# Fewer tokens through the dense experts: 342 dense columns for 352, three chunks between heads for four, one transfer for preactivations and gates

## The chip, the cores and the metric

The kernel runs on one core of a Trainium2 chip. The metric is the device time of one execution in microseconds (us); the number given for a kernel is the median of its runs. PE is TensorE, DVE VectorE, ACT ScalarE, POOL GpSimd and SP SyncE.

## What is computed

One layer of a decoder over 512 tokens of width 2048, in float32. A combined projection feeds latent attention and a spatial gating unit; their output is added to the residual stream h. Then come 16,384 single-neuron experts chosen by product keys, a gated projection of layer inputs, and a last norm. The experts take two thirds of the time:

```python
def peer(a, w_q, k1, k2, u_exp, v_exp):           # a = rmsnorm(h), 512 tokens
    q = (a @ w_q)                                  # 8 heads, two halves of 128
    t1, i1 = top_k(q[first half] @ k1.T, 16);  t2, i2 = top_k(q[second half] @ k2.T, 16)
    top, sel = top_k(t1[:, None] + t2[None, :], 16)
    experts, gates = index(i1 * 128 + i2, sel), softmax(top)   # 8 heads x 16 picks a token
    return sum_k(gates * gelu(u_exp[experts] . a) * v_exp[experts])
h = h + sigmoid(rmsnorm(h) @ W_gate) * (p @ W_ple)
```

## The kernel before, in words

Activations lie transposed, tokens along the free dimension. Each float32 operand is split into a high and a low part (aH and aL, wH and wL), and each product is three matmuls (lines 1745 to 1747). Weights come in pieces of 1 MB: SP loads them into raw, ACT makes wH (line 626), DVE makes wL = raw - wH (line 1048), both in two buffers. A 128 x 2048 piece is a slot of 48 matmuls.

The tokens are handled in three ways. The first TD = 352 go through all experts densely: 128 u chunks of 128 experts each (one slot each, matmuls of 352 columns), then the values in NGROUPS = 16 groups of GROUP = 8 chunks, one group being eight slots. For these tokens a table gates in HBM holds one gate for each expert and token; POOL fills it with zeros early (line 507, 22 transfers) and adds the gates of each head by indirect transfers of one column (line 540, 48 for a head, 384 in all). DVE scales a finished u chunk into ut (line 1472), ACT applies gelu and stores it to pre in HBM. For the values SP loads the chunk and its gates (two transfers, pre_in and gate_in), POOL multiplies (line 585), ACT and DVE split it into actH (line 882) and actL (line 1580).

The last 128 tokens (A) and the 32 before them (B) go by rows instead: for each pick the rows of u and v of one expert a token are gathered, 128 rows at once. The 32 tokens of B are laid out in four sets on the 128 partitions, so that their 128 picks make 32 (B_PICKS), 160 with the 128 of A. Picks below U_PICKS = 64 fall in the u stage, where one gather brings u and v (line 557, 2 MB); the others in the value stage (lines 569 and 577, 1 MB each). For each pick DVE forms the dot product with the token's activations (line 1552; those of A lie in PSUM, those of B in SBUF as b_tok), ACT applies gelu and the gate (lines 899 and 903), and DVE adds the weighted row of v to hT (line 1563) or to b_acc (line 1568). u_step and v_step give each chunk or slot its share of these operations, two to a pick. In the u stage POOL issues four adds of gates after each gather; ADDS_FIRST = 164 adds precede the first one.

The order of each engine's work is written out by hand and engines wait on semaphores. In the head stage a head has two slots of query projection (512 columns), key scores, and HEAD_U = 4 u chunks; DVE's retrieve interleaves the top-16 searches with wL and the scaling. After the heads come 96 more u chunks; picks begin at chunk FIRST_PICK = ROUTE_U + 4 and, but for the last four, end before chunk LAST_PICK = 118. In the value groups ACT seeds PSUM with h (seed) and brings it back (unload); in the first and last group DVE adds PSUM to h (accumulate, line 1585). In the last group PE waits for all picks behind its first slot, transposes the rows of A back, sums the four sets of B by a product with sel behind the second, and squares for the ple norm follow on ACT and DVE. The projection of p (16 tiles) and the gate tiles end the kernel.

Of the kernel before, what the change touches and what calls it, by code (L numbers as in the profile page):

```python
# [22 lines left out]
P = 128  # L23
# [12 lines left out]
BT = 32  # L36
TA = T - P
TD = TA - BT
# [3 lines left out]
B_PICKS = A_PICKS // SETS  # L42
# [10 lines left out]
FIRST_SLOT = 2  # L53

# [8 lines left out]
def v_step(g, q):  # L63

    slots = GROUP * (NGROUPS - 1) - FIRST_SLOT
    return 2 * U_PICKS + max(0, GROUP * g + q - FIRST_SLOT) * 2 * (PICKS - U_PICKS) // slots
# [37 lines left out]
NSLOTS = _n  # L104

# [47 lines left out]
def trunk_layer(nc, a, stream, out, gates_dram, pre_dram):  # L153
# [59 lines left out]
    projT = at("projT", [KD, T], F, W0 + 16 * KB)
# [29 lines left out]
    gates_r = at("gates_r", [NT, P], F, C0)  # L243
    idx_d = at("idx_d", [NTD, P], U32, C0 + 2 * KB)
    idx_s = at("idx_s", [P], U32, C0 + 2 * KB + 1536)
    pre_in = [at(f"pre_in{i}", [TD], F, C0 + 2 * KB * i) for i in range(2)]
    gate_in = [at(f"gate_in{i}", [TD], F, C0 + 4 * KB + 1536 * i) for i in range(2)]
# [6 lines left out]
    gates_b = at("gates_b", [B_PICKS], F, C0 + 14 * KB + 1472)  # L254
    dots_b = at("dots_b", [B_PICKS], F, C0 + 12 * KB + 704)
    pick_wb = at("pick_wb", [B_PICKS], F, C0 + 14 * KB + 1600)
    sel = at("sel", [BT], F, C0 + 14 * KB + 1728)
# [17 lines left out]
    with ctx:  # L275
# [34 lines left out]
        pre_loaded = [sem(f"pre_loaded{i}") for i in range(2)]  # L310
# [7 lines left out]
        gates_loaded = [sem(f"gates_loaded{i}") for i in range(2)]  # L318
# [4 lines left out]
        row_landed = [sem(f"row_landed{i}") for i in range(5)]  # L323
        v_row_landed = [sem(f"v_row_landed{i}") for i in range(2)]
        dot_done, dot_gelu, pick_weighed, pick_done = sem("dot_done"), sem("dot_gelu"), sem("pick_weighed"), sem("pick_done")
        b_loaded, rep_ready, b_tok_done, b_tok_early, b_tok_ready = (
# [1892 lines left out]
```

## Time and profile before

| | us |
|---|---|
| Median of 3 runs (lowest, highest) | 3009.12 (2995.46, 3012.29) |
| The profiled execution, its own time | 2995.07 |
| Its span, first to last instruction | 2992.9 |
| PE busy | 2950.2 (99%) |
| PE loading weights | 2771.6 (93%) |
| DVE busy | 2220.2 (74%) |
| POOL busy | 1435.3 (48%) |
| ACT busy | 1255.1 (42%) |

The core moved 798.01 MB, 267 GB/s over the span. The granted clock of TensorE was 0.998 of its full 2.4 GHz. Busy time of PE counts any moment with a matmul under way; matmuls overlap, so the sum of their durations is larger than it. A row's number with "<-" behind "idle before" names what ended the idle time.

### The profile page before, as it was taken

The page shows a single profiled execution, that of the slowest core. Times are in us where ns is not written, and L with a number is a line of the kernel's source. Part 1 is how long each engine was busy: PE and PEld are TensorE (multiplying, and loading weights), DVE is VectorE, ACT ScalarE, POOL GpSimd, SP SyncE. Part 2 cuts the span into 40 slices and gives each one's busy share as a digit, 9 for nine tenths or more (in the row PEclk, how much of TensorE's full clock was granted, in tenths as well). Part 3 has the DMA queues.
Part 4 walks back from the last instruction along what each step waited for, and adds up shares of the span by engine and source line. Part 5 has one row for each costly group of instructions (what it writes and reads, how often), then busy time and mean ns, then how long its engine had stood idle before and what let it go on. Part 6 is the DMA issues. An engine that isn't in the chain of part 4 may idle for free. (4 is left out here: it accounts for less than half of the span.)

```text
span 2992.9 us, 43288 instructions
## 1 busy us (share of the span) xinstructions
PE 2950.2 (99%) x16888; PEld 2771.6 (93%) x16888; DVE 2220.2 (74%) x2801; ACT 1255.1 (42%) x1818; POOL 1435.3 (48%) x813
## 2 busy tenths in 40 slices
PE   9999999999999999999999999999999999999998
PEld 7888668889999999999999999999999999999787
DVE  5465664578878777777777669888888888986445
ACT  5224542333333333333333334555555555554422
POOL 1010000008888888888888125665555667660000
PEclk9999999999999999999999999999999999999999
DMA  8462222235445599999999889999999999994222
GB/s 297 169 241 86 71 85 98 99 123 125 128 125 137 132 338 339 361 354 364 358 349 362 329 306 412 406 410 403 407 410 408 402 407 401 400 381 152 97 96 99
DMA packets 205172, 798.01 MB, mean 267 GB/s; under 512 B 68208, under 2 KB 121472, under 8 KB 128736
## 3 DMA queue, kind: packets, MB, share of 16 engines
q1 hardware_dynamic: 90768, 405.36, 36.2%
q0 software_dynamic: 95440, 367.63, 34.0%
q10 hardware_dynamic: 18816, 23.11, 2.2%
q8 instruction: 85, 1.39, 0.2%
q14 instruction: 63, 0.52, 0.0%
HBM read 745.46 MB, written 50.51 MB: 266 GB/s over the span
## 5 line engine op out<-in xcount | busy, mean ns | idle before, releaser
L1745 PE MATMUL ps<-aH,wH 128*128 128x352 f32 (+2 forms) x3088 | 1062.0, 344 | 6.9 <-DVE wL L1048 6.9
L1747 PE MATMUL ps<-aH,wL 128*128 128x352 f32 (+2 forms) x3088 | 1059.1, 343 | 0.0
L1746 PE MATMUL ps<-aL,wH 128*128 128x352 f32 (+2 forms) x3088 | 1059.0, 343 | 0.0
L1048 DVE TENSOR_TENSOR wL<-raw,wH 128x2048 fp32r<-128x2048 f32 x333 | 787.5, 2365 | 224.6 <-ACT wH L626 221.9
L540 POOL DMA_INDIRECT gates<-gates_r,idx_d x384 | 753.9, 1963 | 377.9 <-DVE gates_r L1463 243.0
L626 ACT ACTIVATE wH<-raw 128x2048 fp32r<-128x2048 f32 x333 | 636.8, 1912 | 677.2 <-PE ps L1747 581.2
L1745 PE MATMUL ps<-actH,wH 128*128 128x352 f32 x2048 | 662.2, 323 | 3.2 <-DVE wL L1048 3.2
L1747 PE MATMUL ps<-actH,wL 128*128 128x352 f32 x2048 | 661.9, 323 | 0.0
L1746 PE MATMUL ps<-actL,wH 128*128 128x352 f32 x2048 | 661.4, 323 | 0.0
L1745 PEld LDWEIGHTS ps<-aH,wH 128*128 128x128 f32 x3088 | 581.2, 188 | 47.8 <-DVE wL L1048 6.6
L1747 PEld LDWEIGHTS ps<-aH,wL 128*128 128x128 f32 x3088 | 580.9, 188 | 38.1
L1746 PEld LDWEIGHTS ps<-aL,wH 128*128 128x128 f32 x3088 | 580.3, 188 | 38.4 <-issue 0.7
L1745 PEld LDWEIGHTS ps<-actH,wH 128*128 128x128 f32 x2048 | 385.9, 188 | 4.9 <-DVE wL L1048 4.8
L1746 PEld LDWEIGHTS ps<-actL,wH 128*128 128x128 f32 x2048 | 385.4, 188 | 0.0
L1747 PEld LDWEIGHTS ps<-actH,wL 128*128 128x128 f32 x2048 | 385.4, 188 | 0.0
L585 POOL TENSOR_TENSOR pre_in<-pre_in,gate_in 128x352 f32<-128x352 f32 x128 | 221.9, 1735 | 279.3 <-DMA gate_in<-gates 278.2
L1552 DVE SCALAR_TENSOR_TENSOR rows<-rows,ps 128x2048 f32<-128x2048 f32 x128 | 291.8, 2280 | 26.7 <-DMA rows<-uv_rows,idx_s 20.2
L1563 DVE SCALAR_TENSOR_TENSOR hT<-rows,pick_w,hT 128x2048 f32<-128x2048 f32 x128 | 308.5, 2410 | 0.7 <-ACT pick_w L903 0.7
L1472 DVE TENSOR_TENSOR ut<-ps,rstd 128x352 f32<-128x352 f32 x128 | 67.0, 524 | 152.0 <-PE ps L1747 117.1
L569 POOL DMA_INDIRECT rows<-u_rows,idx_s x64 | 121.1, 1892 | 41.9 <-DVE rows L1552 19.0
L1580 DVE TENSOR_TENSOR actL<-pre_in,actH 128x352 fp32r<-128x352 f32 x128 | 68.0, 531 | 89.4 <-ACT actH L882 67.6
L557 POOL DMA_INDIRECT rows<-uv_rows,idx_s x64 | 82.4, 1288 | 105.2 <-DVE hT L1563 87.9
(273 smaller groups left out, 2433.2 us busy)
## 6 DMA issues: line engine op xcount, KB each, us to landing
raw<-s_pu SPq DMA_DIRECT2D x128, 1024.0 KB
raw<-s_pv SPq DMA_DIRECT2D x128, 1024.0 KB
gates<-zeros POOLq DMA_DIRECT2D x22, 1024.0 KB, 8.6
pre<-ut ACTq DMA_DIRECT2D x128, 176.0 KB
pre_in<-pre SPq DMA_DIRECT2D x128, 176.0 KB
gate_in<-gates SPq DMA_DIRECT2D x128, 176.0 KB
raw<-s_out SPq DMA_DIRECT2D x16, 1024.0 KB
raw<-s_pq SPq DMA_DIRECT2D x16, 1024.0 KB
```

The lines of the kernel that those rows point to most:

```text
L540: pool.indirect_dma_start(out=gates_flat, out_offset=bass.IndirectOffsetOnAxis(ap=idx_d[0:m, t, c:c + 1], axis=0), in_=gates_r[0:m, t, c:c ...
L557: pool.indirect_dma_start(out=rows[ROW_AT[j]][:, :, :].rearrange("p a d -> p (a d)"), out_offset=None, in_=a["uv_rows"], in_offset=bass.In ...
L569: pool.indirect_dma_start(out=rows[ROW_AT[j]][:, 0, :], out_offset=None, in_=a["u_rows"], in_offset=bass.IndirectOffsetOnAxis(ap=ids_of(j) ...
L585: nc.gpsimd.tensor_tensor(pre_in[b][:, :], pre_in[b][:, :], gate_in[b][:, :], ALU.mult).then_inc(act_gated, 1)
L626: A(wH[parity][:, :], raw[at_n][:, :], ACT.Copy).then_inc(hi_ready, 1)
L1048: V.tensor_tensor(wL[parity][:, :], src[:, :], wH[parity][:, :].bitcast(F), ALU.subtract).then_inc(lo_ready, 1)
L1552: V.scalar_tensor_tensor(r3, r3, 1.0, act_of, ALU.mult, ALU.mult, accum_out=d).then_inc(dot_done, 1)
L1563: V.scalar_tensor_tensor(hT[:, :, TA:T], v3, pick_w[:, j:j + 1], hT[:, :, TA:T], ALU.mult, ALU.add).then_inc(pick_done, 1)
L1580: V.tensor_tensor(actL[b][:, j, 0:TD], src[:, :], actH[b][:, j, 0:TD].bitcast(F), ALU.subtract).then_inc(act_wlo, 1)
L1745: mm(out, wh, xh, start=start, stop=False, skip_group_check=skip_group_check)
L1746: mm(out, wh, xl, start=False, stop=False, skip_group_check=skip_group_check)
L1747: return mm(out, wl, xh, start=False, stop=stop, skip_group_check=skip_group_check)
```

## The change

- BT goes from 32 to 42: the B tokens become 42, TD = 342, and 170 tokens go by rows. Three sets of 42 fill 126 partitions, the 128 picks of B make 43 (the last set has 42; idx_b and gates_b are cleared for the missing one). PICKS is 171.
- HEAD_U goes from 4 to 3: 24 chunks lie between the heads, 104 behind them. The weight buffers then alternate by head (slot_at, chunk_at).
- 70 picks in the u stage, ADDS_FIRST = 126. Six picks, the last of A, move behind B's: they lie in the last value group and the first projection tiles (tail_steps, TAIL = 6), the last five in a row buffer of their own.
- gates and pre become one tensor pair in HBM with a pitch of 352 for each; SP brings a chunk's gates and preactivations by one transfer. The zeros cover the whole tensor, 44 transfers.
- The last group is seeded and unloaded by ACT like the others. The sum over B's sets is formed in four of its tiles, in PSUM columns behind the 342. The transposes back move into the second half of the projection, and the ple squares and splits of the last 128 tokens come after them, apart from the rest.
- b_tok is taken out of early columns in two steps behind a wait for the last u chunk; sel is built later; buffers in SBUF are laid out anew.

```diff
-BT = 32
+BT = 42
 TA = T - P
+PW = 352
...
-B_PICKS = A_PICKS // SETS
+B_PICKS = -(-A_PICKS // SETS)
+SPAN = SETS * BT
...
-HEAD_U = 4
+HEAD_U = 3
 ROUTE_U = HEAD_U * HEADS
-ADDS_FIRST = 164
+ADDS_FIRST = 126
 FIRST_PICK, LAST_PICK = ROUTE_U + 4, KEYS - GROUP - 2
-U_PICKS, LATE = 64, 4
+U_PICKS, LATE = 70, 4
+TAIL = 6
 FIRST_SLOT = 2
+MAIN = PICKS - TAIL
+FIRST_B = A_PICKS - TAIL
...
+def tail_steps(h):
+
+    if h < 2:
+        return [2 * MAIN + h]
+    return [2 * (MAIN + h // 3) + h % 3] if h >= 3 and h % 3 < 2 and h // 3 < TAIL else []
...
-    _at = _j % 3 if _j < U_PICKS - LATE else 2 if _j < U_PICKS else 3 + _j % 2
+    if _j < U_PICKS:
+        _at = _j % 3 if _j < U_PICKS - LATE else 2
+    else:
+        _at = 4 - (MAIN - _j) % 2 if _j <= MAIN else 5
...
-                sp.dma_start(pre_in[b][:, :], pre_dram[c, :, :]).then_inc(pre_loaded[b], 16)
-                sp.dma_start(gate_in[b][:, :], gates_rows[:, c, :]).then_inc(gates_loaded[b], 16)
+                sp.dma_start(pair_in[b][:, :], pair_rows[:, c, 0:PW + TD]).then_inc(pair_loaded[b], 16)
...
-            fills = -(-KEYS * TD // 2048)
...
+            fills = KEYS * 2 * PW // 2048
...
-                m = min(P, TD - t * P)
+                m = min(P, PW - t * P)
...
-                    pool.wait_ge(b_tok_ready, 1)
-                if j == A_PICKS:
+                    pool.wait_ge(tile_done, CUM[S0["pv"] - 1])
+                if j == FIRST_B:
                     pool.wait_ge(b_loaded, 32 * SETS)
+                if j == MAIN + 1:
+                    pool.wait_ge(tile_done, CUM[S0["pv"] + GROUP * (NGROUPS - 1) - 1])
...
-                pool.wait_ge(pre_loaded[b], (c - b) * 8 + 16)
-                pool.wait_ge(gates_loaded[b], (c - b) * 8 + 16)
-                nc.gpsimd.tensor_tensor(pre_in[b][:, :], pre_in[b][:, :], gate_in[b][:, :], ALU.mult).then_inc(act_gated, 1)
+                pool.wait_ge(pair_loaded[b], (c - b) * 8 + 16)
+                nc.gpsimd.tensor_tensor(pre_in[b], pre_in[b], gate_in[b], ALU.mult).then_inc(act_gated, 1)
...
+            for j in range(MAIN + 1, PICKS):
+                gather_u(j)
+                gather_v(j)
...
+                if KD * (NGROUPS - 1) + 1 <= v <= KD * (NGROUPS - 1) + 4:
+                    A(ps[:, 4 + k % 4, TD:TD + 4 * BT].rearrange("p (c t) -> p c t", c=4), hT[:, 4 * k - 4:4 * k, TD:TA],
+                      ACT.Copy, scale=0.0)
...
                 act.wait_ge(h_acc, v)
+                if g == NGROUPS - 1 and 1 <= k <= 4:
+                    A(b_sum[:, 4 * k - 4:4 * k, :], ps[:, 4 + k % 4, TD:TD + 4 * BT].rearrange("p (c t) -> p c t", c=4),
+                      ACT.Copy).then_inc(b_copied, 1)
...
-                if KD <= v < KD * (NGROUPS - 1):
+                if KD <= v:
                     unload(v)
-                if KD <= v + 4 < KD * (NGROUPS - 1):
+                if KD <= v + 4 < KD * NGROUPS:
                     seed(v + 4)
...
-                if q == 1:
-                    for r in range(4):
-                        act.wait_ge(back_done, r + 1)
-                        A(hT[:, 4 * r:4 * r + 4, TA:T], ps[:, BACK[r], :].rearrange("p (a b) -> p a b", a=4),
-                          ACT.Copy).then_inc(back_copied, 1)
-                    act.wait_ge(back_copied, 4)
+                for o in tail_steps(2 * q) + tail_steps(2 * q + 1):
+                    if o % 2 == 0:
+                        weigh_pick(o // 2)
...
+                    if (s, m) == (1, 3):
+                        for r in range(4):
+                            act.wait_ge(back_done, r + 1)
+                            A(hT[:, 4 * r:4 * r + 4, TA:T], ps[:, BACK[r], :].rearrange("p (a b) -> p a b", a=4),
+                              ACT.Copy).then_inc(back_copied, 1)
+                    if s == 1 and m >= 4:
+                        for k in range(4 * m - 16, 4 * m - 12):
+                            late_hi(k)
+            A(late_sq[:, :, :], hT[:, :, TA:T], ACT.Square).then_inc(sq_ready, 1)
...
-                scale_chunk(uc + 1, 1, at_n(3))
+                if HEAD_U > 2:
+                    scale_chunk(uc + 1, chunk_at(b, 1), at_n(3))
                 key_indices(h, 1)
                 pair_sums(h)
-                lo(n + 5, 1)
+                if HEAD_U > 2:
+                    lo(n + 5, slot_at(b, 5))
                 pair_maxima(h)
-                scale_chunk(uc + 2, 0, at_n(4))
+                if HEAD_U > 3:
+                    scale_chunk(uc + 2, chunk_at(b, 2), at_n(4))
                 pair_more(h)
-                lo(n + 6, 0)
+                if HEAD_U > 3:
+                    lo(n + 6, slot_at(b, 6))
...
+                for o in tail_steps(2 * q):
+                    pick_step(o)
                 lo(m + 1, (q + 1) % 2)
+                for o in tail_steps(2 * q + 1):
+                    pick_step(o)
...
+                if q == 2:
+                    dve.wait_ge(b_copied, 4)
+                    dve.wait_ge(h_acc, KD * (NGROUPS - 1))
+                    V.tensor_tensor(hT[:, :, TD:TA], hT[:, :, TD:TA], b_sum[:, :, :], ALU.add).then_inc(b_added, 1)
+                    dve.wait_ge(b_added, 1)
...
+            for h in range(16, 3 * TAIL):
+                for o in tail_steps(h):
+                    pick_step(o)
+            lo(S0["gate"], 0)
+            for k in range(KD):
+                late_lo(k)
+            n = N_SQ["ple"] + KD
+            dve.wait_ge(sq_ready, n + 1)
+            dve.wait_ge(sq_added, n)
+            V.tensor_reduce(ssum[:, TA:T], late_sq[:, :, :].rearrange("p k t -> p t k"), AX, ALU.add).then_inc(sq_added, 1)
+            lo(S0["gate"] + 1, 1)
...
-                seeded = 0 < g < NGROUPS - 1
+                seeded = g > 0
...
+                    if g == NGROUPS - 1 and 1 <= k <= 4:
+                        if k == 1:
+                            pe.wait_ge(pick_done, MAIN)
+                            pe.wait_ge(sel_ready, 1)
+                        for c in range(4):
+                            t = TD + c * BT
+                            ins = mm(ps[:, 4 + k % 4, t:t + BT], b_acc[:, 4 * k - 4 + c, :], sel[:, :], start=False, stop=True,
+                                     skip_group_check=True)
...
-                if q == 0:
-                    pe.wait_ge(pick_done, PICKS)
-                    for k in range(KD):
-                        ins = nc.tensor.transpose(ps[:, BACK[k // 4], (k % 4) * P:(k % 4 + 1) * P], hT[:, k, TA:T], ident[:, :])
-                        if k % 4 == 3:
-                            ins.then_inc(back_done, 1)
-                if q == 1:
-                    pe.wait_ge(back_copied, 1)
-                    pe.wait_ge(sel_ready, 1)
-                    for k in range(KD):
-                        ins = mm(ps[:, BACK[0], k * BT:(k + 1) * BT], b_acc[:, k, :], sel[:, :], start=True, stop=True)
-                    ins.then_inc(b_sum_done, 1)
-
...
+                    if (s, m) == (1, 3):
+                        pe.wait_ge(pick_done, PICKS)
+                        for k in range(KD):
+                            ins = nc.tensor.transpose(ps[:, BACK[k // 4], (k % 4) * P:(k % 4 + 1) * P], hT[:, k, TA:T], ident[:, :])
+                            if k % 4 == 3:
+                                ins.then_inc(back_done, 1)
+            pe.wait_ge(back_copied, 4)
+            tile(S0["gate"], 0, 0, waits=N_SC["ple"] + KD)
+            norm_sum("ple", 2)
             tile(S0["gate"] + 1, 1, 1)
```

## Rows read from the trace of the kernel before

**Rows 1.** Windows: us; PE, PEld, DVE, ACT, POOL busy; clock; DMA share, GB/s
```profile
620.00:1040.00 420.00, 420.00 (x2392) 393.61 (x2393) 346.56 (x1111) 140.44 (x145) 310.19 (x156) 1.00 0.49 130
1040.00:1400.00 360.00, 358.95 (x2243) 358.66 (x2242) 275.44 (x200) 125.36 (x162) 301.32 (x167) 1.00 0.98 345
1780.00:2200.00 420.00, 417.78 (x2607) 417.05 (x2606) 361.47 (x254) 226.61 (x382) 235.57 (x142) 1.00 1.01 405
2715.00:2775.00 60.00, 59.01 (x383) 58.60 (x381) 38.20 (x46) 32.22 (x40) 0.00 (x0) 1.00 0.34 118
2775.00:2800.00 25.00, 22.73 (x96) 17.89 (x97) 15.16 (x15) 16.08 (x23) 0.00 (x0) 1.00 0.29 101
```

**Rows 2.** Timeline of PE (start, us): first and last of 57, 27, 27 matmuls
```profile
2929.78 0.39 PE L1745 MATMUL ps<-aH,wH 128*128 128x512 f32 x1
...
2942.47 0.39 PE L1747 MATMUL ps<-aH,wL 128*128 128x512 f32 x1
...
2199.70 0.32 PE L1746 MATMUL ps<-actL,wH 128*128 128x352 f32 x1
...
2203.86 0.32 PE L1745 MATMUL ps<-actH,wH 128*128 128x352 f32 x1
...
2964.77 0.28 PE L1745 MATMUL ps<-aH,wH 128*128 128x256 f32 x1
...
2967.89 0.28 PE L1747 MATMUL ps<-aH,wL 128*128 128x256 f32 x1
```

**Rows 3.** Groups of instructions by line and shape, whole span
```profile
L1745 PE MATMUL ps<-actH,wH 128*128 128x352 f32 x2048 | 662.2, 323 | 3.2 <-DVE wL L1048 3.2
L1745 PE MATMUL ps<-aH,wH 128*128 128x352 f32 x2048 | 662.1, 323 | 2.9 <-DVE wL L1048 2.9
...
L507 POOL DMA_DIRECT2D gates<-zeros x22 | 19.6, 890 | 69.0 <-DMA gates<-zeros 68.7 <-POOL zeros L499 0.3
...
L1585 DVE TENSOR_TENSOR hT<-hT,ps 128x352 f32<-128x352 f32 x32 | 16.0, 514 | 7.9 <-PE ps L1747 7.8
```

**Rows 4.** Timeline of DVE where the head loop turns
```profile
817.17 0.23 DVE L1432 CAST best_kf<-best_k 128x128 f32<-128x128 uint32 x1
820.58 0.52 DVE L1472 TENSOR_TENSOR ut<-ps,rstd 128x352 f32<-128x352 f32 x1 [3.18 <-issue]
```

**Rows 5.** Timeline of ACT (ScalarE) there
```profile
827.17 0.60 ACT L850 ACTIVATE pqT<-ps 128x512 f32<-128x512 f32 x1 [5.53 <-PE ps L1747]
```

**Rows 6.** Groups of POOL's instructions from 1200 to 1640 us
```profile
L540 POOL DMA_INDIRECT gates<-gates_r,idx_d x168 | 321.6, 1914 | 57.1 <-issue 50.8 <-DMA gates<-gates_r,idx_d 6.3
L557 POOL DMA_INDIRECT rows<-uv_rows,idx_s x42 | 50.5, 1204 | 12.8 <-issue 12.8
```

**Rows 7.** Waits of DVE from 1060 to 1705 us: us in total, times, longest
```profile
DVE rows L1552 <- DMA rows<-uv_rows,idx_s: 19.3, 16, 3.7
```

**Rows 8.** Timeline of POOL, three adds of gates
```profile
1165.60 2.46 POOL L540 DMA_INDIRECT gates<-gates_r,idx_d  x1 [0.30 <-issue]
1168.36 1.55 POOL L540 DMA_INDIRECT gates<-gates_r,idx_d  x1 [0.30 <-issue]
1170.21 3.30 POOL L540 DMA_INDIRECT gates<-gates_r,idx_d  x1 [0.30 <-issue]
```

**Rows 9.** Timeline of DVE over the same stretch
```profile
1164.33 2.28 DVE L1048 TENSOR_TENSOR wL<-raw,wH 128x2048 fp32r<-128x2048 f32 x1
1166.54 2.28 DVE L1552 SCALAR_TENSOR_TENSOR rows<-rows,ps 128x2048 f32<-128x2048 f32 x1
...
1169.76 2.35 DVE L1563 SCALAR_TENSOR_TENSOR hT<-rows,pick_w,hT 128x2048 f32<-128x2048 f32 x1
```

**Rows 10.** Timeline of POOL: transfer after the zeros, first add, first gather
```profile
327.79 0.57 POOL L521 DMA_DIRECT2D hT<-x  x1 [108.81 <-DVE qT L1247]
...
674.14 1.67 POOL L540 DMA_INDIRECT gates<-gates_r,idx_d  x1 [242.95 <-DVE gates_r L1463]
...
1060.98 1.01 POOL L557 DMA_INDIRECT rows<-uv_rows,idx_s  x1 [0.30 <-issue]
```

More of the change, by code:

```diff
@@ L104, with slot_at, chunk_at @@
 NSLOTS = _n
+def slot_at(b, j):
+    return ((2 + HEAD_U) * b + j) % 2
+def chunk_at(b, j):
+    return (HEAD_U * b + j) % 2
 def raw_at(n):
@@ L309, in trunk_layer @@
         pre_stored = [sem(f"pre_stored{i}") for i in range(2)]
-        pre_loaded = [sem(f"pre_loaded{i}") for i in range(2)]
+        pair_loaded = [sem(f"pair_loaded{i}") for i in range(2)]
         g_scaled = sem("g_scaled")
@@ L392, in _, with load_head @@
                     load(S0["out"] + 2 * i + j, stream["out"][2 * i + j, :, :], j)
-            def load_head(h):
+            def load_head(h, b):
                 n = S0["head"] + (2 + HEAD_U) * h
                 for s in range(2):
-                    load(n + s, stream["pq"][2 * h + s, :, :], s)
+                    load(n + s, stream["pq"][2 * h + s, :, :], slot_at(b, s))
                 for s in range(HEAD_U):
-                    load(n + 2 + s, stream["pu"][HEAD_U * h + s, :, :], s % 2)
-            with sp.Fori(0, HEADS) as h:
-                load_head(h)
+                    load(n + 2 + s, stream["pu"][HEAD_U * h + s, :, :], slot_at(b, 2 + s))
+            with sp.Fori(0, HEADS // 2) as i:
+                for b in range(2):
+                    load_head(2 * i + b, b)
             nu = S0["pu"] - ROUTE_U
@@ L881, in weight_hi @@
                 act.wait_ge(act_gated, c + 1)
-                A(actH[b][:, j, 0:TD], src[:, :], ACT.Copy).then_inc(act_whi, 1)
+                A(actH[b][:, j, 0:TD], src, ACT.Copy).then_inc(act_whi, 1)
             u_beat(ROUTE_U, 0, nu + ROUTE_U, 0)
@@ L965, in v_beat, with dense_square @@
                 turn(KD * g + 2 * q)
+            def dense_square(k):
+                act.wait_ge(h_acc, KD * (NGROUPS - 1) + k + 1)
+                act.wait_ge(sq_added, N_SQ["ple"] + k - 1)
+                A(sq[k % 2][:, 0:TA], hT[:, k, 0:TA], ACT.Square).then_inc(sq_ready, 1)
+                A(aH[:, k, 0:TA], hT[:, k, 0:TA], ACT.Copy, scale=gain("ple", k)).then_inc(act_hi, 1)
             for q in range(GROUP):
@@ L2016, in head_slots @@
                         pe.wait_ge(pq_copied, 2 * h + s - 1)
-                    tile(n + s, s, s, waits=N_SC["ffn"] if first and s == 0 else None)
+                    tile(n + s, slot_at(b, s), s, waits=N_SC["ffn"] if first and s == 0 else None)
                     if first:
@@ L2031, in head_slots @@
                                 ins.then_inc(b_tok_done, 1)
-                    u_slot(n + 2 + s, s % 2, HEAD_U * h + s, s, first=first and s == 1)
+                    u_slot(n + 2 + s, slot_at(b, 2 + s), HEAD_U * h + s, chunk_at(b, s), first=first and s == 1)
             head_slots(0, 0, first=True)
```

231 lines of the change are left out of this document (125 added, 106 removed).

## The prediction

> **What bounds the kernel now.** I read the page first, then the windows by stage. [rows 1] put the stages side by side: the eight heads with four chunks each (620 to 1040 us), the 96 other u chunks (to 1780), the value groups, of which the last ends at 2775, and the projection. The reader is to see that PE is busy for all of 420 us in the heads, for 358.95 of 360 in the u chunks and 417.78 of 420 in the value groups: PE bounds them all. But three others stand close behind. DVE is at 83% in the heads and at 86% in the value groups, POOL at 84% in the u chunks, and the DMA share is 0.98 there and 1.01 in the value groups. So the question is less what PE saves than who can follow it.
>
> **What PE saves.** The timeline of PE gives a matmul's price by the distance of starts, not by its duration, since neighbours overlap [rows 2]. 512 columns: 2929.78 to 2942.47 over 56 distances, 226.6 ns. 352 columns: 4.16 us over 26, 160.0 ns. 256 columns: 3.12 us over 26, 120.0 ns. A column costs (226.6 - 120.0)/256 = 0.416 ns; 256 plus 96 columns gives 160.0, which is the middle row, so the line is straight. 342 columns make 155.8 ns. [rows 3] count 2048 matmuls with aH and 2048 with actH at 352 columns, and each stands for three: 12,288. Times 4.17 ns that is **-51.2 us**. A slot of 48 goes from 7.68 to 7.48 us. Below nothing this can't go; it is nothing if columns cost in blocks of 32, which the three shapes (all multiples of 32) don't exclude.
>
> PE's work for the 42 split tokens stays: 16 products with sel and 16 transposes before and after, in other places.
>
> **Heads (three chunks between two).** No chunk is dropped, only moved behind the heads, so PE pays the same. A head gets shorter by one slot and three times 0.2, 8.3 us; DVE sheds one wL (2.28) and one scaling (about 0.5). At the end of a head it is then 5.5 us further behind PE. Now it ends a head at 817.40, waits 3.18 us for issue where its loop turns, scales a chunk from 820.58 [rows 4] and then has wL (2.28) written at 823.3; PE needs that at 827.17, where ScalarE sees the first query tile end [rows 5]: 3.9 us to spare. So it comes 1.6 us late in the three turns of the loop, and elsewhere, without the 3.18, in time: **+4 us** (0 to 10; DVE has 73 us idle in 420 now [rows 1], half of it left).
>
> **POOL between 1040 and 1780.** This is the term that decides. It issues one gather (2 MB) for each pick and four adds of gates. In 440 us of steady work [rows 6] it did 168 adds of 1.914 us and 42 gathers of 1.204 with 70 us between them, nearly all "issue": 442 us, it never rests. That is 440/42 = 10.5 us for a pick. Today's plan spreads 60 picks over 82 slots of 7.68, one in 10.5 us: a tie, and [rows 7] show it as a tie, DVE waiting 16 times for rows in the whole stage (19.3 us, none longer than 3.7, hidden in its own idle time). The new plan spreads 66 picks over 90 slots of 7.48, one in 10.2 us, still with four adds each (258 adds are left after the first 126, so they last for 64.5 picks, the whole stage). POOL is short of 0.3 us in each pick.
>
> Why POOL is so slow is in the two timelines [rows 8, 9]. An add takes 1.55 us under the dot product of 1166.54, which reads one input from PSUM. The one of 1165.60 takes 2.46: wL runs until 1166.61, which leaves 1.45. The one of 1170.21 takes 3.30: the row addition runs until 1172.11, which leaves 1.40. So an instruction of POOL that starts under a DVE operation with two SBUF inputs waits for its end. The Trainium skill, "GPSIMD Engine Reference", section Specifications, says that its SBUF interfaces contend with DVE instructions that have two SBUF inputs; the trace agrees, with the 2.46 and 3.30 against 1.55.
>
> The price: the lead that POOL has at the start is about one pick (two gathers go before the first adds) and DVE may be some 3 us late before PE feels it, together 13 us. Loss = 64 x (p - 10.2) - 13 for a pace of p. At today's p = 10.53 (4 x 1.914 + 1.204 + 5 x 0.305 + a rare wait for the adds of a head) 8 us. With the adds at the 2.36 us that they take apart in the heads (674.14 to 1060.98 for 164 [rows 10]) p = 10.95, 35 us. I take p = 10.65, **+16 us**, nearer to the stage's own rows but above them, as the DVE operations with two SBUF inputs take the same 4.0 us out of a shorter slot. It ends with the adds, at about the 116th of 128 chunks.
>
> **The zeros.** 44 fills instead of 22, the 22 new ones behind the others. A fill costs POOL 0.9 us and 3.1 of waiting (19.6 + 69.0 over 22 [rows 3]), so they take 89 us, and POOL idles there for 108.81 us before its next transfer [rows 10]. That idle time is the cover. **0 us**, to 3 without cover.
>
> **The value groups.** One transfer for two leaves 128 packets of 2776 B for 256 of 1408 B. POOL, ACT and DVE do as much as before with 3% fewer columns. Bytes for a slot: 405 GB/s x 7.68 us = 3.11 MB now [rows 1]; some 0.02 MB less after, for 165 picks of which 95 lie in 118 slots. 3.09 MB in 7.48 us are 413 GB/s. What the queues can carry beyond 405 no row shows; cost from 0 to, if 405 is the most, 118 x (7.63 - 7.48) = 18 us. I take **+2**, since PE lost only 2.2 us in 420 at 405 GB/s and a share of 1.01. The Trainium skill, "DMA: Bandwidth & Descriptors", puts the ceiling of the SBUF fabric at 435 GB/s, and a core's share of HBM at about 358. The first would leave the stage free, the second would forbid even now's 405; the trace decides against the second.
>
> **The end.** Six picks (12 operations of 2.28 or 2.35) move into the last group; ACT takes over 16 additions of 0.51 [rows 3]; squares and low parts shrink by a quarter of some 12 us. DVE had 38.20 of 60 us [rows 1]: 38.2 + 28 - 8.2 - 3 = 55, of 59.8, with more than a slot's 7.48 bunched in slots 2, 3 and 6. A late wL there costs 2 to 3 us. Behind, the transposes move from slot 1 of the group to the middle of the projection, where they wait for the last pick; by the plan it comes after eight slots, two squares, a wL and itself, at 70 us of the group, and is wanted after eight slots and twelve tiles of six matmuls, at 76. Queued behind that wait on PE are four projection tiles and the gate. PE now loses 1.0 + 2.3 us there and this partly stays. **+3 us** (-2 to 12).
>
> **Sum.** The profiled execution took 2995.07 us (span 2992.9, 2.2 around it): 2995.1 - 51.2 + 4 + 16 + 0 + 2 + 3 = 2969.9. The median of the runs is 14 us above that execution. A part of this may be the very race of POOL and DVE, already counted; I carry 6 over: **2976 us**.
>
> **Rivals.**
> - *All of the saving arrives.* POOL's stalls fall so that it follows at 10.2. For it: an unhindered add takes 1.55 and a gather 1.0, 8.7 us in all. Against it: [rows 6], where it had every reason to be faster and wasn't. 2995 - 51 + 9 = 2953, to 2962 with the shift of the median. Chance 0.2.
> - *DMA is the bound in the value groups* on top of my case: +16 more, 2992. For it a share of 1.01; against it PE's 417.78 of 420 at that share. 0.1.
> - *Slower: POOL falls out of step.* A start at random finds DVE in such an operation for 54% of a slot, with half of 2.3 us to wait: 0.6 us for each of five instructions, p = 8.7 + 3.0 = 11.7, a loss of 83 us in place of 16: 3043. It decides (over 3024) from p = 11.4. For it: the alignment that gives 10.5 belongs to slots of 7.68. Against it: waiting behind an operation is itself what aligns. 0.1. A pace between 10.9 and 11.3 leaves 2990 to 3020, no change: 0.05.
> - *The columns don't count singly* (blocks of 32): no gain, and no loss on POOL either as the slots stay: 2995 + 5 + 6 = 3006. 0.05.
>
> **How the numbers follow.** My case has 0.5, from 2955 to 2992. A measurement of this kernel can tell about 0.5%, 15 us around 3009: faster is below 2994. Faster: 0.47 of mine, 0.2 and 0.03 of the DMA case, 0.70. Slower: 0.10. No change: 0.20. The range that leaves 2 in 10 outside is 2950 to 3010; it takes in the free case below and most of the no-change cases above.
>
> **What the profile after would show.** Distances of 155.8 ns at 342 columns. Between the last head and the last eight u chunks, PE losing 10 to 20 us where it now loses 3, behind wL, with DVE waiting for rows far more than 19.3 us and POOL still without rest at 10.5 to 10.8 us for a pick. In the value groups a GB/s of about 410 and slots of 7.5. A loss of 1 to 2 us in each turn of the head loop. Wrong would be: no wait of PE in the u stage at all (free case), slots of 7.6 in the value groups (DMA), over 11.3 us for a pick (slower), or distances of 160.

## The result, and the profile after

The changed kernel took 3010.98 us (median of 20 runs, 3003.15 to 3023.38), the one before, measured side by side with it, 3001.12 (20 runs, 2995.25 to 3012.29): ratio 1.0032, 95% interval 1.0022 to 1.0042. That is 10 us slower: a small loss, but the interval leaves 1 out. It lies above my 2976 and above the upper end of my range, 3010. The profiled execution of after took 3012.23 us (span 3010.5) against 2995.07 (span 2992.9): 17 us more.

Busy time of the engines in the changed kernel (from here on: after), and then its windows in the order of [rows 1]:
```profile
PE 2935.2 (98%) x16888; PEld 2752.4 (91%) x16888; DVE 2270.8 (75%) x2836; ACT 1270.5 (42%) x1898; POOL 1481.4 (49%) x853
```
```profile
620.00:1040.00 420.00, 412.00 (x2358) 383.90 (x2357) 364.56 (x1130) 143.02 (x153) 278.69 (x145) 1.00 0.52 148
1040.00:1400.00 360.00, 350.44 (x2196) 349.77 (x2195) 273.66 (x192) 121.08 (x159) 289.33 (x164) 0.99 0.98 346
1780.00:2200.00 420.00, 418.19 (x2648) 417.41 (x2647) 361.56 (x256) 222.37 (x376) 240.53 (x138) 1.00 0.99 403
2715.00:2775.00 60.00, 59.35 (x386) 59.06 (x385) 52.05 (x45) 41.48 (x79) 14.40 (x10) 1.00 0.79 298
2775.00:2800.00 25.00, 21.53 (x109) 19.04 (x108) 19.87 (x22) 14.01 (x27) 4.43 (x2) 0.93 0.58 211
```
PE was busy all of the heads and 358.95 of 360 us in the u chunks; now it is idle for 8 of 420 and 9.56 of 360. The value groups are as full as before. So the loss lies ahead of 1780 us. Who is late there, from the waits of 1060 to 1705 us (total, times, longest), which answer to [rows 7]:
```profile
DVE rows L1632 <- DMA rows<-uv_rows,idx_s: 65.6, 26, 10.0
...
POOL pair L576 <- DMA pair<-gates_r,idx_d: 31.7, 4, 9.8
...
PE ps L1851 <- DVE wL L1121: 25.6, 6, 7.4
```
PE waits for wL, DVE before it for gathered rows, and POOL, which issues the gathers, for adds of gates: four times here and a fifth time before 1591.39, 10.85 us that the view puts under "issue" though they stand at the same place of the program:
```profile
1591.39 2.82 POOL L576 DMA_INDIRECT pair<-gates_r,idx_d  x1 [10.85 <-issue]
```
That makes five waits of 6.5 to 10.8 us, 42.5 in all. POOL's groups from 1200 to 1640 us, beside [rows 6]:
```profile
L576 POOL DMA_INDIRECT pair<-gates_r,idx_d x161 | 303.9, 1888 | 76.6 <-issue 59.0 <-DMA pair<-gates_r,idx_d 17.6
L594 POOL DMA_INDIRECT rows<-uv_rows,idx_s x41 | 50.5, 1232 | 12.5 <-issue 12.5
```
An add takes 1.888 us, 1.914 before; what has grown is the wait for adds, from 6.3 to 28.4 (17.6 and the 10.8 that stand under "issue"). For a gather with its adds POOL takes (303.9 + 76.6 + 50.5 + 12.5)/41 = 443.5/41 = 10.8 us.

Where the 17.6 us of span went, from the starts of PE's matmuls. I call a distance of starts above 0.6 us, less the 0.16 of a matmul, a hole, and the excess over 0.16 of those from 0.27 to 0.6 slow. Stages in us; holes and slow in brackets:
```
           heads, from     u chunks, to     value groups   last group,
           606 us on       the first value  0 to 14        projection, gate
before     429.2 (2, 0)    744.5 (3, 0)     927.2 (4, 0)   275.6
after      372.7 (9, 1)    829.6 (30, 9)    912.8 (3, 1)   279.0
```
The chunk that left each head's gap reappears in the u stage, so the first two stages go together: 1173.7 before, 1202.3 after, **+28.6**. Value groups **-14.4**, the rest **+3.4**; sum 17.6.

One of the four long holes (of 4.9, 5.0, 7.6 and 5.0 us; each follows one of the last four waits), at the start of the seventh head's adds. Timeline of POOL (start, us, engine, operation, in brackets the idle time before it and who ended it), then DVE, then PE:
```profile
1442.73 0.99 POOL L594 DMA_INDIRECT rows<-uv_rows,idx_s  x1 [0.31 <-issue]
1444.02 1.45 POOL L576 DMA_INDIRECT pair<-gates_r,idx_d  x1 [0.30 <-issue]
1445.78 1.42 POOL L576 DMA_INDIRECT pair<-gates_r,idx_d  x1 [0.30 <-issue]
1456.99 2.40 POOL L576 DMA_INDIRECT pair<-gates_r,idx_d  x1 [9.78 <-DMA pair<-gates_r,idx_d]
1459.69 3.38 POOL L576 DMA_INDIRECT pair<-gates_r,idx_d  x1 [0.30 <-issue]
1463.37 1.34 POOL L594 DMA_INDIRECT rows<-uv_rows,idx_s  x1 [0.30 <-issue]
```
```profile
1461.57 2.29 DVE L1121 TENSOR_TENSOR wL<-raw,wH 128x2048 fp32r<-128x2048 f32 x1
1473.89 2.29 DVE L1632 SCALAR_TENSOR_TENSOR rows<-rows,ps 128x2048 f32<-128x2048 f32 x1 [10.04 <-DMA rows<-uv_rows,idx_s]
```
```profile
1473.67 0.32 PE L1853 MATMUL ps<-aH,wL 128*128 128x342 f32 x1
1481.39 0.65 PE L1851 MATMUL ps<-aH,wH 128*128 128x342 f32 x1 [7.40 <-DVE wL L1121]
1481.84 0.49 PE L1852 MATMUL ps<-aL,wH 128*128 128x342 f32 x1
1482.12 0.49 PE L1853 MATMUL ps<-aH,wL 128*128 128x342 f32 x1
```
The code says `if h >= 1: pool.wait_ge(gates_added[(h - 1) % 2], ...)` before the first of a head's 48 adds: all adds of the head before must have landed. The last two of them stand in POOL's queue (q0) behind the gather issued at 1442.73 (2 MB). The DMA packets show it: the gather's 128 of 16,384 bytes start between 1446.01 and 1452.12 us, and the 240 small ones of the two adds only between 1451.39 and 1455.61. In the window 1446 to 1451 (packets, MB, share of 16 engines):
```profile
q0 software_dynamic: 199, 1.87, 99.1%
```
Until the adds land, POOL issues nothing for 9.78 us; the next gather leaves at 1463.37 and lands ten microseconds later, DVE stands for 10.04, PE for 7.40. The Trainium skill, "DMA: Bandwidth & Descriptors", section Queues, rings and completion order, says of the queues of SP and ACT that a DMA engine takes the descriptors of a ring in order. The queue here is POOL's; its packets come in the same order, as the starts above show.

The windows show what follows the hole:
```profile
1475.00:1485.00 10.00, 3.61 (x13) 3.61 (x14) 9.83 (x9) 5.58 (x8) 8.48 (x6) 0.57 0.84 267
1485.00:1500.00 15.00, 15.00 (x92) 15.00 (x92) 9.31 (x8) 3.60 (x5) 12.90 (x7) 0.95 1.01 365
```
After PE's 7.4 us at rest the granted clock is 0.57 in this window, mostly the lower level of 1.2 GHz, and the matmuls start 0.28 us apart instead of 0.158. Those behind the four holes are nearly all of the 9 us of slow.

### The profile page after: what moved, and what is told of

It reads as the page before. It is cut to its first block, busy times and chain, and to the rows that moved or that the text cites. A ratio compares the mean times of both kernels' runs of the same rounds, so it can differ in the third digit from the quotient of the medians.

```text
span 3010.5 us, 43195 instructions
## 1 busy us (share of the span) xinstructions
PE 2935.2 (98%) x16888; PEld 2752.4 (91%) x16888; DVE 2270.8 (75%) x2836; ACT 1270.5 (42%) x1898; POOL 1481.4 (49%) x853
## 4 chain that ended last, share of the span: by engine, by line
PE 64%; POOL 17%; DVE 8%; issue 5%; DMA 3%; ACT 2%; ACTq 0%; DVEq 0%; SPq 0%; POOLq 0%
PE ps L1851 21%; PE ps L1852 20%; PE ps L1853 20%; POOL pair L576 15%; POOL rows L594 3%; DVE wL L1121 2%; DMA pair<-gates_r,idx_d 2%; ACT wH L667 1%; DVE rows L1632 1%; PE ps L2049 1%; PE ps L2105 0%; PE ps L2026 0%; DMA pair_in<-pair 0%; DMA raw<-s_pu 0%; DVE hT L1644 0%
## 5 line engine op out<-in xcount | busy, mean ns | idle before, releaser
L1851 PE MATMUL ps<-aH,wH 128*128 128x342 f32 (+2 forms) x3088 | 1064.3, 345 | 40.7 <-DVE wL L1121 40.7
L1852 PE MATMUL ps<-aL,wH 128*128 128x342 f32 (+2 forms) x3088 | 1057.5, 342 | 0.0
L1853 PE MATMUL ps<-aH,wL 128*128 128x342 f32 (+2 forms) x3088 | 1052.9, 341 | 0.0
L576 POOL DMA_INDIRECT pair<-gates_r,idx_d x384 | 738.2, 1922 | 398.4 <-DVE gates_r L1536 234.9
L1851 PE MATMUL ps<-actH,wH 128*128 128x342 f32 x2048 | 661.1, 323 | 3.1 <-DVE wL L1121 2.9
L1852 PE MATMUL ps<-actL,wH 128*128 128x342 f32 x2048 | 655.1, 320 | 0.0
L1853 PE MATMUL ps<-actH,wL 128*128 128x342 f32 x2048 | 649.0, 317 | 0.0
L623 POOL TENSOR_TENSOR pair_in<-pair_in 128x342 f32<-128x342 f32 x128 | 210.9, 1649 | 212.6 <-DMA pair_in<-pair 211.5
L1545 DVE TENSOR_TENSOR ut<-ps,rstd 128x342 f32<-128x342 f32 x128 | 65.8, 514 | 136.4 <-PE ps L1853 121.1
L942 ACT ACTIVATE dots<-dots 128x1 f32<-128x1 f32 x128 | 25.5, 199 | 303.5 <-DVE rows L1632 259.0
```

The costliest lines, as they stand in the source:

```text
L576: pool.indirect_dma_start(out=gates_flat, out_offset=bass.IndirectOffsetOnAxis(ap=idx_d[0:m, t, c:c + 1], axis=0), in_=gates_r[0:m, t, c:c ...
L623: nc.gpsimd.tensor_tensor(pre_in[b], pre_in[b], gate_in[b], ALU.mult).then_inc(act_gated, 1)
L1545: V.tensor_tensor(ut[b][:, :], ps[:, 6 + b, 0:TD], rstd[:, 0:TD], ALU.mult).then_inc(chunk_scaled, 1)
L1851: mm(out, wh, xh, start=start, stop=False, skip_group_check=skip_group_check)
L1852: mm(out, wh, xl, start=False, stop=False, skip_group_check=skip_group_check)
L1853: return mm(out, wl, xh, start=False, stop=stop, skip_group_check=skip_group_check)
```

## The experiments

**1. Two adds more among the heads.** 126 adds are issued among the heads and each pick takes four, so it is fixed how many adds of a head's 48 stand behind the last gather when the next head's first add waits. With (144 - 126) mod 4 = 2 it is two; the kernel before had (192 - 164) mod 4 = 0.
```diff
-ADDS_FIRST = 126
+ADDS_FIRST = 128
```


> The changed kernel with 128 instead of 126 adds before the first gather, so that a head's first add comes straight behind a gather and not two adds behind it. Theory 1 (the head boundary): the four waits of POOL for the previous head's adds fall from 6.5 to 9.8 us to the 3.1 to 4.2 of the kernel before, the 5 to 8 us holes of PE in the u stage go, and the kernel gains 20 to 35 us on the changed one (2975 to 2990 us). Rival 2 (the general pace of POOL): the rate over the stage stays short of the plan, holes move to other places, gain under 8 us. Rival 3 (the transfers of the new tensor are slower): no change.


2990.56 us (10 runs), ratio to before 0.9972 (0.9957 to 0.9988): 20 us less for one constant. The expected range ended at 2990. POOL's waits for adds, from 1060 to 1705 us:
```profile
POOL pair L576 <- DMA pair<-gates_r,idx_d: 14.2, 4, 4.4
```
42.5 us in five waits became 14.2 in four (at the first of the five places POOL hardly waits now), the longest 10.8 became 4.4. The u stage took 807.3 us, holes 13, slow 4.

**2. The same the other way round, in the kernel before.**
```diff
-ADDS_FIRST = 164
+ADDS_FIRST = 166
```


> The kernel before with 166 instead of 164 adds before the first gather: its head boundaries now lie two adds behind a gather, and nothing else changes. Theory 1: the three to four waits grow from 3.1 to 4.2 to 6.5 to 10 us, and as its plan has no reserve either PE gets holes of 3 to 5 us: 10 to 25 us slower. Rival 2: POOL's pace is what counts and two adds are nothing: no change (under 3 us).


3026.57 us (4 runs), ratio 1.0084 (1.0055 to 1.0113), 26 us above before's median and a little more than expected. The waits at the heads' first adds became 7.1, 9.4, 6.4 and 11.2 us. The u stage went from 744.5 to 772.4, with holes of 22 and slow of 7. The same two adds harm a kernel that has none of the change.

**3. Is it the place or the number of adds?** Two more counts, of which only the second is a multiple of four from 144.
```diff
-ADDS_FIRST = 126
+ADDS_FIRST = 130        (and, in another kernel, 132)
```


> The kernel after, with 130 instead of 126 adds in the stage of the heads (the run at 128 took 2990.6 us, 0.9972 of before; after itself 1.0032). My theory, the place of a head's last adds in the queues: 144-130 = 14 is again 2 more than a multiple of four, so the last two adds of a head stand in queue 0 behind a gather of 2 MB, GpSimd waits 6.5 to 9.8 us at each of the four turns of the heads in the stage of the first group (30 us in all, as at 126; 14 at 128), and the time is within 6 us of after: 3003 to 3013. Rival, the number of adds left to the stage: each add more among the heads takes one from the 24-add rhythm behind, so 130 is better than 128: 2982 to 2990, with waits at the turns of 4 us or less.

> The kernel after with 132 adds among the heads. By the place in the queues 144-132 = 12 is a multiple of four, as with 128: waits of GpSimd at the turns of the heads 3 to 4.5 us, 14 in all, time 2984 to 2992. By the rival (only the number of adds matters) it would be below both 128 and 130, by as much again as those two differ.


130: 3010.62 us, ratio 1.0032 (1.0014 to 1.005), u stage 824.3 (holes 27, slow 8), as slow as 126 with four adds fewer left. 132: 2988.17, ratio 0.9953 (0.9933 to 0.9972), 795.7 (6, 0). One turn at 130, with the gather and the two adds behind it again:
```profile
1438.38 0.99 POOL L594 DMA_INDIRECT rows<-uv_rows,idx_s  x1 [0.30 <-issue]
1439.68 2.76 POOL L576 DMA_INDIRECT pair<-gates_r,idx_d  x1 [0.30 <-issue]
1442.74 1.86 POOL L576 DMA_INDIRECT pair<-gates_r,idx_d  x1 [0.30 <-issue]
1451.12 2.04 POOL L576 DMA_INDIRECT pair<-gates_r,idx_d  x1 [6.51 <-DMA pair<-gates_r,idx_d]
```
At 130 all five waits are there (6.5 to 9.1 us, 37 in all). The place decides. What the number does besides is less sure: the medians at 128 and 132 differ by 2 us, but in the profiled executions the u stage took 12 us less with 132 (795.7 against 807.3).

**4. What a width costs.** The kernel before, with another number of columns in the matmuls of each value group from 1 to 14; the tokens behind it lack that group's share. It ran once, so each width was seen in one stretch of one execution.
```diff
+WIDTH = [352, 350, 348, 346, 344, 342, 340, 338, 336, 334, 332, 330, 328, 324, 320, 352]
-three(ps[:, 4 + k % 4, 0:TD], ..., actH[b][:, c, 0:TD], actL[b][:, c, 0:TD],
+n = WIDTH[g]
+three(ps[:, 4 + k % 4, 0:n], ..., actH[b][:, c, 0:n], actL[b][:, c, 0:n],
```


> The kernel before with the matmuls of value groups 1 to 14 cut to 350, 348, 346, 344, 342, 340, 338, 336, 334, 332, 330, 328, 324 and 320 columns (the tokens behind them lack that group's share). If columns count singly, the mean distance of starts falls by 0.83 ns for every two columns, from 160.0 to 146.7 ns. If a width that is no multiple of some block costs more, the distances form steps: for blocks of 32 nothing below 352 is gained until 320; for blocks of 8 or 16 the means at 344 and 336, or at 336 and 320, lie on the line and those between above it. At 342 the changed kernel shows 158.0.


Mean distance of starts in a group (363 to 383 distances below 0.2 us), beside the line of [rows 2], 13.3 + columns/2.4:
```
columns   352   350   348   346   344   342   340   338   336   334   332   330   328   324   320
ns      160.4 160.0 158.3 159.5 157.8 157.8 155.0 153.3 153.4 151.2 150.3 152.1 149.3 149.1 146.6
line    160.0 159.2 158.3 157.5 156.7 155.8 155.0 154.2 153.3 152.5 151.7 150.8 150.0 148.3 146.7
```
One pair of starts for 342 and one for 340, 51 distances apart each:
```profile
2139.97 0.32 PE L1746 MATMUL ps<-actH,wH 128*128 128x342 f32 x1
...
2148.03 0.32 PE L1746 MATMUL ps<-actH,wH 128*128 128x342 f32 x1
...
2199.76 0.32 PE L1746 MATMUL ps<-actH,wH 128*128 128x340 f32 x1
...
2207.66 0.32 PE L1746 MATMUL ps<-actH,wH 128*128 128x340 f32 x1
```
8.06/51 = 158.0 ns and 7.90/51 = 154.9. The rival of blocks of 32 is dead, and so is my straight line: in this execution 340 and 336 lie on it, 342 and 346 2 ns above, 334 and 332 1.3 below. In the kernel after the starts tell the same, 8.04/51 = 157.6:
```profile
2198.03 0.33 PE L1851 MATMUL ps<-actH,wH 128*128 128x342 f32 x1
...
2206.07 0.32 PE L1851 MATMUL ps<-actH,wH 128*128 128x342 f32 x1
```
The price at 342 is firm: in every kernel with 342 columns the mean distance is 157.8 ns, in the u chunks as in the value groups. Two other widths have two prices each. At 344 the next experiment has both 153.3 and 157.8 ns; at 352 the kernels have 160.0 in some stretches and 161.1 in others, the second for instance in the value groups of experiment 6 (8.21/51 = 161.0):
```profile
2199.83 0.32 PE L1851 MATMUL ps<-actH,wH 128*128 128x352 f32 x1
...
2208.04 0.32 PE L1851 MATMUL ps<-actH,wH 128*128 128x352 f32 x1
```
So a width with one stretch in the table may have another price too, and the table alone can't tell. What chooses between the two no run shows.

**5. 344 columns in the whole kernel**, with 128 adds, so against experiment 1.
```diff
-BT = 42
+BT = 40
```


> The kernel at 128 adds (2990.6 us), with 40 instead of 42 tokens whose value rows are gathered, so that the blocks of the value groups have 344 columns and not 342. By a price that goes straight with the columns, 2 more are 0.83 ns x 12,288 matmuls = 10 us more: 3001. By the distances measured width by width (344: 157.8 ns, 342: 157.8 to 158.0) they are free: 2988 to 2993, and the distance in the value groups is 157.5 to 158.2 ns.


2987.14 us, ratio 0.9947 (0.993 to 0.9965), against 2990.56 with 342 columns, measured at another time (0.9972, 0.9957 to 0.9988). In the value groups, starts at 2201.21 and, 51 later, 2209.26: 157.8 ns. By the straight line two more columns are 10 us; they were free. In the u chunks about a third of the slots were cheaper still, 7.82/51 = 153.3 ns:
```profile
1381.73 0.32 PE L1853 MATMUL ps<-aH,wL 128*128 128x344 f32 x1
...
1389.55 0.32 PE L1853 MATMUL ps<-aH,wL 128*128 128x344 f32 x1
```

**6. Only the layout.** The changed kernel with the old sizes: one transfer for preactivations and gates, the new last picks and buffers, but 352 columns, 32 tokens and four chunks.
```diff
-BT = 42
+BT = 32
-HEAD_U = 3
+HEAD_U = 4
-ADDS_FIRST = 126
+ADDS_FIRST = 164
-U_PICKS, LATE = 70, 4
+U_PICKS, LATE = 64, 4
```


> The changed kernel with the numbers of the kernel before (32 B tokens, 352 columns, four chunks a head, 64 picks in the u stage, 164 adds first), so that the one transfer for preactivations and gates, the 44 fills, the six late picks and the new end stand alone. If the loss lies in those parts it is as slow as the changed kernel, over 3005. Theory 1 with the columns: those parts cost or give at most 5 us and it lies within 5 us of the kernel before.


3002.02 us, ratio 1.0000 (0.9985 to 1.0014). The u stage is 744.5 us, as before. Value groups +4.0 (931.2), last group -2.1 (66.6), projection and gate +4.4 (26.5 and 184.8). The +4.0 is the second price of 352 columns: the mean distance in the value groups was 161.0 ns here and 160.2 in before, 0.8 x 5760 = 4.6 us. That leaves no cost of the layout there.

**7. The 42 tokens with four chunks in a head.**
```diff
-HEAD_U = 3
+HEAD_U = 4
-ADDS_FIRST = 126
+ADDS_FIRST = 164
-U_PICKS, LATE = 70, 4
+U_PICKS, LATE = 64, 4
```


> The changed kernel (342 columns) with four chunks a head again, 64 picks in the u stage and 164 adds first, aligned with the heads as before. Theory (the heads of three chunks cost 7 us, DVE comes late where its loop turns): the three holes of 2 to 3 us in the head stage go, the u stage keeps a small shortage (60 picks in 82 slots of 7.58 us, 10.36 us for a pick against POOL's 10.5), 4 to 12 us faster than the changed kernel with 128 adds (2990.6). Rival (101 picks in the value stage instead of 95 make DMA or DVE the bound there): the value stage grows by over 10 us and takes it back.


2992.2 us (10 runs, 2983.93 to 3005.02), ratio 0.9968 (0.9944 to 0.9992): no gain on experiment 1, against my theory, though the three holes in the heads are gone as it said. Heads and u stage together 1162.8, 11 less than before. But six picks more than in after fall to the value groups, and those took 928.1 us with 16 us of holes, 0.9 more than before: the 13.8 us that their columns save are given back there, as the rival said.

**8. Fewer picks in the u stage.** 128 adds and 68 picks; then 136 and 66.
```diff
-ADDS_FIRST = 126
+ADDS_FIRST = 128        (136)
-U_PICKS, LATE = 70, 4
+U_PICKS, LATE = 68, 4   (66)
```


> The changed kernel with 128 adds first and 68 instead of 70 picks in the u stage: 64 in 90 slots of 7.58 us, one in 10.66 us, which is more than the 10.5 that POOL takes, where 66 gave 10.34. Theory of the pace: the 13 us of holes that are left in the u stage go, and it gains about 10 us on the kernel with 70 (2990.6), the value stage paying up to 3 us for two more picks. Rival (what is left there are the waits of a head's first add alone, which stay at 3 to 4 us each whatever the plan): no gain.

> The changed kernel with 66 picks in the u stage (62 in 90 slots, one in 11.0 us) and 136 adds first, still aligned. By the pace theory nothing is left of the u stage's holes, as with 68, and the value stage carries 99 picks: bytes for a slot 3.16 MB, 417 GB/s at slots of 7.58 us. If DMA is near its end there, the value stage grows by 5 us or more against 68 picks; if not, it equals that kernel within 3 us.


68: 2976.43 us, ratio 0.9912 (0.9888 to 0.9936). 66: 2984.93, ratio 0.9936 (0.9911 to 0.9961). The u stage took 791.7 and 791.4 us with 2 us of holes in each, so 68 is already enough; the value groups 914.7 and 920.2. The 5.5 us more are what I had named as the sign that DMA is near its end there; what PE waited for is DVE's wL. PE's waits from 1790 to 2710 us at 66 picks, and then at the 64 of experiment 7:
```profile
PE ps L1851 <- DVE wL L1121: 8.3, 9, 1.7
```
```profile
PE ps L1851 <- DVE wL L1121: 13.5, 18, 1.7
```
With 68 they were 3.4 us. At 68 DVE no longer waits for rows between 1060 and 1705 us; POOL waits for it instead:
```profile
POOL rows L594 <- DVE hT L1644: 22.9, 10, 6.6
...
POOL pair L576 <- DMA pair<-gates_r,idx_d: 10.6, 3, 3.8
```
The pace that the plan asks for tells why. A slot is 48 x 157.8 ns = 7.57 us, and 66, 64 or 62 picks are spread over 90 slots: 10.3, 10.6 or 11.0 us a pick. POOL needs about 10.5 [rows 6]. The pace is not the whole of it: with 132 adds among the heads and still 70 picks (experiment 3) the u stage had only 6 us of holes.

**9. The head loop of DVE written out** (with 128 adds).
```diff
-            with st.loop(HEADS // 2 - 1, 2 * HEAD_STEPS) as i:
+            for i in range(HEADS // 2 - 1):
```


> The changed kernel with 128 adds first, and DVE's loop over the last six heads written out, so that it doesn't turn: nothing else changes. If the turn's 3.2 us of issue are the cause of the holes, all three go and it gains 6 to 8 us on the same kernel with the loop (2990.6). If DVE is late because its own work in a head of three chunks is too long, the holes stay, perhaps at every head: no gain.


2985.31 us (5 runs), ratio 0.9945 (0.9923 to 0.9968), 5 us below experiment 1, though the intervals of the two ratios overlap. In the profiled executions the holes of the heads fell from 9.2 to 5.2 us. The timeline of DVE at the loop's turn in after, and then without the loop:
```profile
794.30 0.23 DVE L1505 CAST best_kf<-best_k 128x128 f32<-128x128 uint32 x1
797.78 0.52 DVE L1545 TENSOR_TENSOR ut<-ps,rstd 128x342 f32<-128x342 f32 x1 [3.25 <-issue]
```
```profile
793.87 0.23 DVE L1505 CAST best_kf<-best_k 128x128 f32<-128x128 uint32 x1
794.13 0.52 DVE L1545 TENSOR_TENSOR ut<-ps,rstd 128x342 f32<-128x342 f32 x1
```
The 3.25 us are gone, and with them PE's waits of 1.64 and 1.75 us near 800 and 895 us. So two holes went, not three as expected: the loop has three passes and turns back twice. The largest wait there stays, and it is none of the loop:
```profile
701.12 2.26 DVE L1556 TENSOR_TENSOR b_rep<-b_rep,rstd 128x2016 f32<-128x2016 f32 x1
703.29 0.51 DVE L1545 TENSOR_TENSOR ut<-ps,rstd 128x342 f32<-128x342 f32 x1
703.72 2.28 DVE L1121 TENSOR_TENSOR wL<-raw,wH 128x2048 fp32r<-128x2048 f32 x1
```
```profile
706.05 0.50 PE L1851 MATMUL ps<-aH,wH 128*128 128x512 f32 x1 [2.88 <-DVE wL L1121]
```
DVE writes the split tokens' inputs there (two operations of 2.25 us), and with a chunk less in the gap its wL comes 2.88 us late. With four chunks (experiment 7) this hole isn't there.

**10. The three edits together.**
```diff
-ADDS_FIRST = 126
+ADDS_FIRST = 128
-U_PICKS, LATE = 70, 4
+U_PICKS, LATE = 68, 4
-            with st.loop(HEADS // 2 - 1, 2 * HEAD_STEPS) as i:
+            for i in range(HEADS // 2 - 1):
```


> The three edits that helped, together: 128 adds among the heads, 68 instead of 70 picks in the stage of the first group, and the loop over the heads of VectorE written out. If they add up: 2976.4 us of the run with 68 picks less the 5.3 us that writing out gave: 2971, 0.989 to 0.990 of before. Rival: with 68 picks the stage no longer waits for rows, the heads' earlier end moves GpSimd's and the DMA's work too, and PE already stands still for only some 2 us there: the 4 us of the turns alone arrive, or nothing: 2972 to 2977.


2973.27 us (6 runs, 2970.99 to 2975.87), ratio 0.9895 (0.9872 to 0.9918): about 1% faster than before (the medians alone, 2973.27 and 2999.76, give 0.9912), where the change as made is 0.3% slower. It lies 2 us above "all adds up" (2971) and within the rival's 2972 to 2977; the interval is 7 us wide to either side, so this run doesn't decide between the two. In the windows PE is whole again, and the queues carry 413 GB/s in the value groups, where before had 405:
```profile
1040.00:1400.00 360.00, 360.00 (x2283) 360.00 (x2282) 279.34 (x195) 123.75 (x162) 298.19 (x170) 1.00 1.00 358
1780.00:2200.00 420.00, 418.27 (x2648) 417.40 (x2647) 375.38 (x259) 227.07 (x394) 256.45 (x143) 1.00 1.01 413
```

## Why the prediction was wrong, step by step

**Columns: mis-sized.** I said 155.8 ns and -51.2 us. In value groups 0 to 14 the mean distance fell from 160.2 to 157.8 ns (in the u chunks from 160.4): 2.4 x 12,288 = -29. The step that failed is "the line is straight" through three widths that are all multiples of 32: right there, and 2 ns off at 342. It cost 22 us of the forecast. The Trainium skill, "TensorE: Matmul & The Clock Gate", section Wait — 56ns, not 53.3ns?, gives back-to-back matmuls N/2.4 GHz plus a fixed 2.5 ns; no width here does so. The fixed part was 13.3 ns at 320, 336 and 340 columns and 15.3 at 342; at 352 it was 13.3 or 14.4, at 344 10.0 or 14.4. Its rule for the lower clock, N/1.2 GHz, is 285 ns at 342, and the trace agrees: 0.28 and 0.29 after the hole.

**POOL's pace: right mechanism, one wait left out.** I put +16 on the stage and carried "a rare wait for the adds of a head" over as it was. Measured: holes and slow 39.1 us in the u stage against 3.5 before, +36. With 128 adds the same stage has 16.7, +13: this fits the part that I had worked out, the plan asking for a pick sooner than POOL gives it, and experiment 8 takes it away. Its size is unsure, since 132 adds left only 6. The other 22 us are the wait at a head's first add, which the new 126 made long by placing two adds behind a gather. This is the second step that failed: "a rare wait for the adds of a head" was 3.1 and 3.2 us in the window of [rows 6] and became five waits of 6.5 to 10.8. Experiments 1 to 3 turn it on and off by the remainder, in the old kernel too. I had the wait in my sum, and never asked what sets its length. Part of both is the lower clock after a hole, which I had not counted at all.

**Heads: +4 forecast, +7 of holes measured.** Two turns of the loop cost 1.64 and 1.75 us, as forecast (1.6). The third forecast turn doesn't exist: three passes turn back twice, and before shows DVE's stop twice as well, of 3.18 us at 820.58 and 3.22 at 929.31. Missed were the 2.88 us behind the two operations on split tokens at 702 us.

**Zeros: 0, right, but with nothing to spare.** The fills and the transfer behind them:
```profile
L543 POOL DMA_DIRECT2D pair<-zeros x44 | 39.3, 893 | 144.6 <-DMA pair<-zeros 144.3 <-POOL zeros L536 0.3
```
```profile
328.65 0.57 POOL L557 DMA_DIRECT2D hT<-x  x1 [14.95 <-issue]
```
44 fills took 184 us, 95 more than 22 did (89 forecast), and the transfer starts at 328.65 where it started at 327.79 [rows 10]: the 108.81 us of cover are used up to the last 15.

**Value groups: +2 forecast, -0.6 measured.** Their 14.4 us less are the 13.8 of the columns (5760 x 2.4). The slots there are 7.57 us, which I had named as the sign of the DMA rival; it is the width that makes them so. DMA is not the bound at this plan: with two picks more there (experiment 10) the queues carry 413 GB/s, and PE loses under 2 us in 420. But the reserve is small. With four and six picks more (experiments 8 and 7) the stage had 9 and 16 us of holes at 415 and 414 GB/s. PE waited for DVE's wL, and DVE for 5.5 and 8 us for gathered rows; no run separates DVE's own work from the DMA there.

**End: +3 forecast, +3.4 measured.** The number fits, the place only in part: the last group took 0.9 us less than before, so its picks did no harm; the loss lies in projection and gate (+4.3), and experiment 6 has the same with old sizes, so it belongs to the layout. I didn't look further.

**The sum again.** My own was added up wrong by 1: its terms give 2968.9, not 2969.9. With the measured terms, -29 + 7 + 36 + 0 + 3 = +17, and the profiled executions differ by 17.2. The 6 us that I carried from the median were right for before: its median over 20 runs is 3001.1, 6 above its profiled execution. They were not for after, whose median lies 1.2 below its own, and so the medians differ by only 10. From 2976 the forecast missed by 35 us: about 22 are the columns, 20 POOL's stage and 3 the heads, less 2 for the value groups and 7 for that difference between medians and profiled executions. A part of before's spread may be the two prices at 352 columns: 12,288 x 1.1 ns are 14 us between all of one and all of the other, an estimate, since only the profiled executions show which price ran.

**The rivals.** None of them named the wait at the head's turn. "Slower: POOL falls out of step" was wrong in its mechanism: POOL kept 10.8 us a pick, and the adds even took a little less time each. "The columns don't count singly" came nearest in number (3006) by luck: there are no blocks of 32, more than half of the saving arrived, and the loss came from POOL.

## What to carry to other kernels

When a constant shifts where one stream of small transfers is cut against another in the same queue, look at the waits for the last of the small ones: whether two of them stand behind a 2 MB gather was worth 20 us here, two thirds of what the narrower matmuls saved. Ask for each tie between an engine and a plan what pace the new plan wants; where it wants more than the profile has shown, move work (two picks of 171) before saving any. And price a matmul at the width that will be used, not on a line through round ones, and in more than one stretch, since a width can have two prices.

## What had not been expected of the hardware

- The distance of matmuls doesn't follow the columns alone. At 342 it is 157.8 ns in every stretch; at 344 it is 157.8 in some and 153.3 in others, and at 352 160.0 or 161.1. In the one execution with many widths 332 columns took 150.3 ns and 330 took 152.1, but each was seen in one stretch.
- At each of the four holes of 4.9 to 7.6 us PE's granted clock fell: to 0.57 from 1475 to 1485 us, and to 0.68 to 0.83 in the ten microseconds from the end of the others, with starts 0.28 us apart for 9 to 18 matmuls. A hole thus costs more than its length: 9 us on 30.
- DVE's head loop costs 3.2 us at each of its two turns here, idle with nothing waited for that the profile shows; written out, nothing.
